# Rows spread over partitions in one pass: a rounded high part and a low part stacked in 40 rows, instead of full-precision matmuls

## What is computed

```
p = x @ w_in                                # 2048 -> RWKV-7 | retention | mLSTM columns
o_rw  = group_norm(rwkv7_scan(..., kk * rsqrt(sum kk^2 per head), ...)) ...   # 8 heads of 64
o_ret = silu(gr) * (yr * rsqrt(mean yr^2 per head))                           # 6 heads of 128
o_ml  = sigmoid(om) * (hm * rsqrt(mean hm^2 per head)) * ml_norm              # 6 heads of 128
        # mLSTM: exp(dlog - m_i), exp(inter - m_i): one value per head and token
x1 = layernorm(ALPHA * x + concat(o_rw, o_ret, o_ml) @ w_out)
x2 = layernorm(ALPHA * x1 + (silu(x1 @ w_gate) * (x1 @ w_up)) @ w_down)
```

## Time and profile before

| | |
|---|---|
| median of 3 runs | 2909.44 us (2906.31 to 2909.49) |
| profiled execution: time, span | 2905.3 us, 2903.5 us |
| mean granted TensorE clock | 0.975 of full |
| PE busy, PEld busy | 96%, 93% of the span |
| DVE busy, ACT busy | 56%, 41% |
| DMA | 152 GB/s over the span |

### The profile page before, as it was taken

One profiled execution on the slowest core, in us unless ns is written; L12 is line 12 of the kernel. 1 busy time (PEld: TensorE's weight loads), 2 busy tenths in 40 slices (PEclk: granted clock), 3 DMA queues, 4 the chain that ended last, 5 costly groups with the idle time before them and its releaser, 6 DMA issues.

```text
span 2903.5 us, 56248 instructions
## 1 busy us (share of the span) xinstructions
PE 2796.0 (96%) x23683; PEld 2697.5 (93%) x23683; DVE 1615.6 (56%) x1674; ACT 1180.7 (41%) x1455; POOL 0.2 (0%) x4
## 2 busy tenths in 40 slices
PE   6999999999999999999999999999999999999995
PEld 5988898889999999999999999888999999999995
DVE  5546547559554545444585575455875545454444
ACT  4345333436333333333363453343553333333333
POOL 0000000000000000000000000000000000000000
PEclk9999999989999999999999999989999999999997
DMA  5625334436666566555564543342666565655551
GB/s 158 195 85 156 89 89 136 125 112 187 185 177 179 175 180 176 178 179 170 179 196 140 163 114 89 83 131 73 187 188 180 174 181 174 180 179 179 173 181 60
DMA packets 278664, 445.02 MB, mean 153 GB/s; under 512 B 45124, under 2 KB 75646, under 8 KB 278182
## 3 DMA queue, kind: packets, MB, share of 16 engines
q1 hardware_dynamic: 276888, 439.29, 50.8%
q10 hardware_dynamic: 1600, 3.12, 0.3%
HBM read 430.58 MB, written 11.78 MB: 152 GB/s over the span
## 4 chain that ended last, share of the span: by engine, by line
PE 91%; DVE 5%; ACT 3%; issue 1%; DMA 0%; ACTq 0%; DVEq 0%
PE psum L644 19%; PE psum L645 19%; PE psum L643 19%; PE psum L676 7%; PE psum L677 6%; PE psum L678 6%; ACT w_hi L1215 1%; DVE w_lo L1589 1%; PE psum L877 1%; PE psum L666 1%; PE psum L667 1%; PE psum L668 1%; PE psum L867 1%; PE psum L1039 1%; PE psum L1024 1%
## 5 line engine op out<-in xcount | busy, mean ns | idle before, releaser
L1585 DVE TENSOR_TENSOR w_lo<-w_raw,w_hi 128x1024 fp32r<-128x1024 f32 x496 | 606.1, 1225 | 705.5 <-ACT w_hi L1202 703.8
L1202 ACT ACTIVATE w_hi<-w_raw 128x1024 fp32r<-128x1024 f32 x508 | 538.9, 1061 | 929.6 <-PE psum L645 920.4
L643 PE MATMUL psum<-x_hi,w_lo 128*128 128x264 f32 (+3 forms) x3072 | 878.8, 286 | 6.9 <-DVE x_lo L1787 6.9
L645 PE MATMUL psum<-x_hi,w_hi 128*128 128x264 f32 (+3 forms) x3072 | 879.5, 286 | 0.0
L644 PE MATMUL psum<-x_lo,w_hi 128*128 128x264 f32 (+3 forms) x3072 | 878.7, 286 | 0.0
L643 PEld LDWEIGHTS psum<-x_hi,w_lo 128*128 128x128 f32 x3072 | 582.1, 189 | 8.0 <-issue 7.3
L644 PEld LDWEIGHTS psum<-x_lo,w_hi 128*128 128x128 f32 x3072 | 581.3, 189 | 0.2
L645 PEld LDWEIGHTS psum<-x_hi,w_hi 128*128 128x128 f32 x3072 | 580.4, 189 | 0.0
L1589 DVE TENSOR_TENSOR w_lo<-w_raw,w_hi 128x1024 fp32r<-128x1024 f32 x304 | 369.0, 1222 | 247.0 <-ACT w_hi L1215 226.3
L1215 ACT ACTIVATE w_hi<-w_raw 128x1024 fp32r<-128x1024 f32 x292 | 304.9, 1056 | 299.2 <-PE psum L678 236.3
L676 PE MATMUL psum<-x_hi,w_lo 128*128 128x264 f32 (+1 forms) x1376 | 416.0, 302 | 6.3 <-ACT p_ml L1242 4.5
(11 more groups left out here) (444 smaller groups left out, 2605.3 us busy)
## 6 DMA issues: line engine op xcount, KB each, us to landing
w_raw<-in_w_in SPq DMA_DIRECT2D x192, 512.0 KB, 3.7
w_raw<-in_w_gate SPq DMA_DIRECT2D x176, 512.0 KB, 3.7
w_raw<-in_w_up SPq DMA_DIRECT2D x176, 512.0 KB, 3.8
w_raw<-in_w_down SPq DMA_DIRECT2D x176, 512.0 KB, 4.1
w_raw<-in_w_out SPq DMA_DIRECT2D x64, 512.0 KB, 3.9
w_raw<-in_w_in SPq DMA_DIRECT2D x16, 262.0 KB, 2.8
r_sample<-in_state_ret SPq DMA_DIRECT2D x6, 512.0 KB, 8.4
out_s_ret<-r_sample SPq DMA_DIRECT2D x6, 512.0 KB, 5.5
```

What stands on the lines that cost most here:

```text
L643: mm(out, w1, bh[:, k, 0:nt], start=(k == 0), stop=False)
L645: last = mm(out, w0, bh[:, k, 0:nt], start=False, stop=(k == last_k))
L1202: A(wh[:, j, :, :], raw[:, j, :, :], ACT.Copy).then_inc(S.hi_ready, 1)
L1585: TT(wl[:, j, :, :], raw[:, j, :, :], wh[:, j, :, :].bitcast(F32), ALU.subtract).then_inc(S.lo_ready, 1)
```

## The change

The table of selectors gets 40 rows: rows 0 to 7 as before, zeros, and the same eight rows again as rows 32 to 39. It is loaded as `selectors_loaded` and cast once to fp32r by DVE. A set of n rows is now kept twice in a tile of 40 rows: its rounded high part in rows 0 to n-1 and what is left of it in rows 32 to 32+n-1, with zeros between. One fp32r matmul of 38 or 40 rows with the doubled selector gives the sum of both parts in each output. The tile is `row_parts` for the norms and `m_row_parts` (three sets) for the mLSTM's rows. `invert` does the reciprocal, the rounding and the subtraction in turn, each waiting for the one before it. ACT computes two of the exponentials a second time, rounded, as the high parts. Cut to its core, the diff is:

```diff
-    sel = np.zeros((RW_HEADS, AH + 4, 128), f)
+    sel = np.zeros((32 + RW_HEADS, AH + 4, 128), f)
...
+    sel[32:] = sel[0:RW_HEADS]
...
-    sel = put("selectors", [RW_HEADS, AH + 4, 128])
+    sel = put("selectors", [32 + RW_HEADS, AH + 4, 128], F32R)
...
+    parts = at("row_parts", P_END + T * 4, [32 + RW_HEADS, T], F32R)
+    mparts = at("m_row_parts", P_X, [32 + AH, 3, T], F32R)
...
# PE: attention's spread and spread1 (h in 4, AH: the same), kks and gnsp, spread_m, spread_e
-                    last = mm(ps[:, 4 + h, 0:T], sel[0:AH, h, :], ln_s[0:AH, :], start=True, stop=True)
+                    last = mm(ps[:, 4 + h, 0:T], sel[0:32 + AH, h, :], parts[0:32 + AH, :], start=True, stop=True)
...
-                    last = mm(ps[:, 4 + b, 0:T], sel[:, AH + b, :], ln_s[0:RW_HEADS, :], start=True, stop=True)
+                    last = mm(ps[:, 4 + b, 0:T], sel[:, AH + b, :], parts[:, :], start=True, stop=True)
...
-                    last = mm(ps[:, 4 + h // 2, SEQ * (h % 2):SEQ * (h % 2) + SEQ], sel[0:AH, h, :], row(3)[:, 0:SEQ],
+                    last = mm(ps[:, 4 + h // 2, SEQ * (h % 2):SEQ * (h % 2) + SEQ], sel[0:32 + AH, h, :], mparts[:, 0, 0:SEQ],
                               start=True, stop=True)
                 last.then_inc(S.m_spread, 1)
                 bg.to('spread_e')
                 pe.wait_ge(S.m_exp_in, l + 1)
-                pe.wait_ge(S.m_rows_e, l + 1)
+                pe.wait_ge(S.m_rows_x, 2 * l + 2)
...
-                        mm(ps[:, 4 + p, SEQ * i:SEQ * i + SEQ], sel[0:AH, AH + p, :], row(r_)[:, 0:SEQ], start=True, stop=True)
+                        mm(ps[:, 4 + p, SEQ * i:SEQ * i + SEQ], sel[0:32 + AH, AH + p, :], mparts[:, 1 + i, 0:SEQ], start=True, stop=True)
...
# ACT
-                act.wait_ge(S.m_rows_x, l + 1)
+                act.wait_ge(S.m_rows_x, 2 * l + 1)
+                A(mparts[0:AH, 2, :], row(1), ACT.Exp)
                 A(row(1), row(1), ACT.Exp)
+                A(mparts[0:AH, 1, :], row(4), ACT.Exp)
                 A(row(4), row(4), ACT.Exp)
...
# DVE: invert replaces each v.reciprocal of ln_s (L1881, L2003, L2186)
+            def invert(n, sem):
+                x, hi = ln_s[0:n, :], parts[0:n, :]
+                own(v.reciprocal(x, x))
+                own(v.tensor_copy(hi, x))
+                TT(parts[32:32 + n, :], x, hi.bitcast(F32), ALU.subtract).then_inc(sem, 1)
...
+                if l == 0:
+                    dve.wait_ge(S.tables_loaded, 16 * 5)
+                    own(v.tensor_copy(sel[:, :, :], sel_raw[:, :, :]))
...
+                own(TS(parts[0:32, :], masks[0:32, 0:T], 0.0, None, ALU.mult))
                 bg = behind_ret(l)
...
+                own(TS(mparts[0:32, :, :], masks[0:32, 0:3 * T].rearrange("p (a t) -> p a t", t=T), 0.0, None, ALU.mult))
                 bg.to('gn')
...
                 dve.wait_ge(S.m_rows_m, l + 1)
+                then(v.tensor_copy(mparts[0:AH, 0, :], row(3)))
+                then(TT(mparts[32:32 + AH, 0, :], row(3), mparts[0:AH, 0, :].bitcast(F32), ALU.subtract))
                 then(TT(row(2), row(2), row(3), ALU.add))
...
+                dve.wait_ge(S.m_rows_e, l + 1)
+                TT(mparts[32:32 + AH, 1, :], row(4), mparts[0:AH, 1, :].bitcast(F32), ALU.subtract)
+                TT(mparts[32:32 + AH, 2, :], row(1), mparts[0:AH, 2, :].bitcast(F32), ALU.subtract).then_inc(S.m_rows_x, 1)
                 bg.to('spread_m')
```

More of the change, by code:

```diff
@@ L116, in constants @@
     return {'c_base': base, 'c_ident2': ident2, 'c_masks': masks, 'c_rot': rot, 'c_ret': ret, 'c_gam': gam,
-            'c_sel': sel.reshape(RW_HEADS, -1), 'c_sums': sums}
+            'c_sel': sel.reshape(32 + RW_HEADS, -1), 'c_sums': sums}
 def build(nc, a, o):
@@ L284, in build @@
     x_tok = at("x_rows", 0, [128, 3, D])
+    sel_raw = at("selectors_loaded", P_RW, [32 + RW_HEADS, AH + 4, 128])
     y_tok = at("y_rows", 0, [128, 3, D])
@@ L898, in attention @@
                 for h in range(4, AH):
-                    last = mm(ps[:, h, 0:T], sel[0:AH, h, :], ln_s[0:AH, :], start=True, stop=True)
+                    last = mm(ps[:, h, 0:T], sel[0:32 + AH, h, :], parts[0:32 + AH, :], start=True, stop=True)
                 last.then_inc(S.a_spread, 1)
@@ L1135, in _ @@
                 pe.wait_ge(S.rw_out, l + 1)
-                pe.wait_ge(S.m_rows_x, l + 1)
+                pe.wait_ge(S.m_rows_x, 2 * l + 1)
                 for c in range(NCH):
@@ L1144, in _ @@
                 pe.wait_ge(S.m_exp_in, l + 1)
-                pe.wait_ge(S.m_rows_e, l + 1)
+                pe.wait_ge(S.m_rows_x, 2 * l + 2)
                 for p in range(AP_):
-                    for i, r_ in enumerate((4, 1)):
-                        mm(ps[:, 4 + p, SEQ * i:SEQ * i + SEQ], sel[0:AH, AH + p, :], row(r_)[:, 0:SEQ], start=True, stop=True)
-                        last = mm(ps[:, 7, 16 * p + 8 * i:16 * p + 8 * i + 8], sel[0:AH, AH + p, :], row(r_)[:, SEQ:T],
+                    for i in range(2):
+                        mm(ps[:, 4 + p, SEQ * i:SEQ * i + SEQ], sel[0:32 + AH, AH + p, :], mparts[:, 1 + i, 0:SEQ], start=True, stop=True)
+                        last = mm(ps[:, 7, 16 * p + 8 * i:16 * p + 8 * i + 8], sel[0:32 + AH, AH + p, :], mparts[:, 1 + i, SEQ:T],
                                   start=True, stop=True)
@@ L1256, in _ @@
             act.dma_start(gam[:, :], a['c_gam']).then_inc(S.tables_loaded, 16)
-            act.dma_start(sel[:, :, :].rearrange("p a b -> p (a b)"), a['c_sel']).then_inc(S.tables_loaded, 16)
+            act.dma_start(sel_raw[:, :, :].rearrange("p a b -> p (a b)"), a['c_sel']).then_inc(S.tables_loaded, 16)
             act.dma_start(sums[:, :], a['c_sums']).then_inc(S.tables_loaded, 16)
@@ L1440, in _ @@
                 act.wait_ge(S.rw_kk_ss, l + 1)
-                A(ln_s[0:RW_HEADS, :], ln_m[0:RW_HEADS, :], ACT.Sqrt).then_inc(S.rw_kk_norm, 1)
+                A(ln_s[0:RW_HEADS, :], ln_s[0:RW_HEADS, :], ACT.Sqrt).then_inc(S.rw_kk_norm, 1)
                 for b in range(4):
@@ L1880, in attention @@
                 dve.wait_ge(S.a_std, n + 1)
-                v.reciprocal(ln_s[0:AH, :], ln_s[0:AH, :]).then_inc(S.a_inv, 1)
+                invert(AH, S.a_inv)
                 bg.to('spread')
@@ L2000, in _ @@
                 dve.wait_ge(S.rw_kk_sq, l + 1)
-                TS(ln_m[0:RW_HEADS, :], ps[0:RW_HEADS, 4, 0:T], 1e-24, None, ALU.max).then_inc(S.rw_kk_ss, 1)
+                TS(ln_s[0:RW_HEADS, :], ps[0:RW_HEADS, 4, 0:T], 1e-24, None, ALU.max).then_inc(S.rw_kk_ss, 1)
                 dve.wait_ge(S.rw_kk_norm, l + 1)
-                v.reciprocal(ln_s[0:RW_HEADS, :], ln_s[0:RW_HEADS, :]).then_inc(S.rw_kk_inv, 1)
+                invert(RW_HEADS, S.rw_kk_inv)
                 dve.wait_ge(S.rw_kk_raw, l + 1)
@@ L2185, in _ @@
                 dve.wait_ge(S.rw_gn_std, l + 1)
-                v.reciprocal(ln_s[0:RW_HEADS, :], ln_s[0:RW_HEADS, :]).then_inc(S.rw_gn_inv, 1)
+                invert(RW_HEADS, S.rw_gn_inv)
                 bg.to('gnsp')
```

## The result

| | median | runs | profiled execution: time, span | clock |
|---|---|---|---|---|
| before | 2907.86 us | 5 (2902.57 to 2909.49) | 2905.3, 2903.5 | 0.975 |
| changed | 2889.12 us | 5 (2884.76 to 2891.22) | 2889.2, 2887.5 | 0.977 |

The changed kernel is faster: ratio 0.9935, 95% interval [0.9923, 0.9947], which is 18.7 us by the medians. The forecast was 19.4 us less, a median of 2890 us.

A forecast was written before the change was run, and what follows sets the result against it. PE was taken to bound the kernel, busy 96% of the span. Savings of 7.54 us per layer, 15.1 in two, plus 4.3 from the clock gave 19.4 less: a median of 2890 us, range 2878 to 2902.

The forecast's parts named there:

- What bounds the kernel: PE, busy 96% of the span: a microsecond saved there counts, except where PE soon stands still for another engine.
- The price of a rounded matmul: At all six spreads: 0.122 us for each fp32r selector matmul, as for the filler's, instead of 0.492 in fp32.
- The additions: `invert` adds some 0.8 us, two ACT exponentials 0.64; zeroing and the table's cast cost nothing on the path.
- Retention: Retention's spreads: 1.25 us saved per layer, about 0.4 of `spread`'s 1.48 and all 0.85 of `spread1`.
- kks, 0: At kks: PE gains only 0.7 us, lost again at its next wait, L971, so 0 per layer.
- gnsp, -0.1: At gnsp: later ACT exponentials delay L2189 by 0.1 to 0.2 us, PE waits for `p_ml`; -0.1 per layer.
- spread_m, spread_e: The mLSTM's row spreads: no PE wait near, so the full 2.04 and 2.87 us per layer are saved.
- mLSTM: mLSTM's attention: `spread` saves 1.48 us per layer; `spread1`'s 0.85 only lengthens PE's wait for L666.
- The clock, 4.3: Three half-clock stretches behind spread_m and spread_e would be gone with the shorter fp32 runs, saving 4.3 us.
- The signs of being wrong: Selector matmuls of 0.25 us or more, half-clock stretches where none were, or PE waiting for `w_lo` in the filler.
- the clock gives nothing back: Rival, chance 0.19: longer waits open as many half-clock stretches as are won, leaving 15.1 us saved, 2894.

The follow-up runs named there:

- rows_128: The changed kernel with selectors and row sets filled up with zeros to 128 rows: 2886.10 us, ratio 0.9935 to the kernel before.
- adds_only: The kernel before plus all the change's additions on DVE and ACT, every selector matmul left fp32: 2907.44 us against 2905.87, ratio 1.0005.
- before_later_lo: The kernel before with one `w_lo` of DVE behind kks in layer 0 issued later, nothing else: 2899.33 us against 2908.21, ratio 0.9978.
- repeated: The changed kernel with each selector matmul of spread_m and spread_e issued four times: 2911.21 us against 2908.21 for the kernel before, ratio 1.0017.
- no_kks: The changed kernel with kks alone left in fp32, without its additions: 2889.37 us, ratio 0.9942 to the kernel before.
- later_lo_no_kks: The changed kernel with layer 0's `w_lo` behind kks issued later and kks in fp32 without additions: 2880.85 us against 2908.21 before, ratio 0.9915.
- later_lo: The changed kernel with one `w_lo` of DVE behind kks in layer 0 issued later: 2884.82 us against 2908.21 before, ratio 0.9930.
- rwkv_only: The kernel before with only kks and gnsp in the rounded format: 2910.89 us against 2905.87, ratio 1.0018.

## Why the prediction was right

- **What bounds the kernel**: right. PE's own stream decides, and a saving counts unless PE waits soon after.
- **The price of a rounded matmul**, 0.122: right within a run (0.12), too low at its ends. The first and last of a run take 0.22 and 0.21 to the next start; `rows_128` shows that this is the change between 128 and 40 rows. Four cost 0.67 and not 0.49, spread_m's six 0.90 and not 0.73. spread_e's twelve cost 1.47 and not 1.15, the larger part of it because a pair with an 8-column matmul takes 0.23 and not the estimated 0.19. Together this is most of the 1.7 us between 15.1 and 13.4.
- **The additions**: 0.78 for `invert` (0.8 taken), hidden at the attentions, on PE's path at kks (0.65 of wait), and `adds_only` bears out that all of them together cost little (1.6 us by the medians, at most 4 by the interval).
- **Retention**: 1.13 and 1.16 of 1.25, with the new wait at L903 (0.72 where 1.1 was expected).
- **kks, 0**: right in both layers, and the wait grew at the place named. But I took the longer wait to be free, and in layer 0 it wasn't: the half clock moved from ahead of it to behind it and took 0.86. The missing stretch at 309 gave 1.3 back, which the new wait of 1.26 at L1003 took again, so the retention's 0.85 was gone. No term stood for that.
- **gnsp, -0.1**: right in both layers, by the way predicted (two exponentials, then `w_hi`, `w_lo`, L2210).
- **spread_m, spread_e**: right but for the price above.
- **mLSTM**: right in size. The saving of `spread1` (0.64) is lost at L1159, which waits 0.59 us for `o_lo`, a step ahead of the L670 that I had named; L670's own wait is unchanged at 2.23.
- **The clock, 4.3**: the three stretches are gone, and they gave 1.5, 1.6 and some 1.5 us, so the step was right, though its reason was only half right: a long run of selector matmuls, not the fp32 format. What it left out is that others come and go. In the first profile 6.2 us were won behind spread_m and spread_e (with a fourth stretch at 1951), 5.3 lost in the four rows of the table with "none", and 1.7 won outside the table; in the second profile of the same program the balance is 4.4 us better. The forecast of 4.3 lies between 2.6 and 7.0, and that it came out right within a microsecond owes something to chance.
- **The signs of being wrong**: one of the three came true. Half-clock stretches turned up where none were, behind L670 in both layers, at 624.3 and 2023.8. They are not clearly the change's doing: the wait there is 2.23 us in both kernels, and `adds_only` and `before_later_lo`, in which every selector matmul is fp32, have half clock there in layer 0 as well (from 631.4 and 625.1).

The rival "the clock gives nothing back" (15.1 us) is the one that the first profile comes nearest to. The Trainium skill, "TensorE: Matmul & The Clock Gate", section "HAM oscillation", lays the throttling to idle time between bursts. Here a half-clock stretch does stand behind the waits of 5.25 and 2.23 us; that at 528.7 in `repeated` has no idle time ahead of it, and behind the 2.23 us of the kernel before there is none, so the rule is not the whole of it.

**What stays open.** Why the parts don't add up (8.2 against 18.7 us), and why `no_kks` is no faster than the whole while `later_lo_no_kks` is faster than `later_lo`. Totals of half clock differ from kernel to kernel by more than the effects of a place, and two profiles of one program by 10 us, so I take it for the clock; no run shows it. Nor is it shown what costs `rwkv_only` its 5 us.

## What to carry to other kernels

Before a saving on the busiest engine is counted, look for its next wait and follow that chain to its head: if the head is not the place that gets faster, the saving is gone, and a longer wait can even cost a little clock (0.6 to 0.8 us here). Such a chain can be worth more than the instruction: moving one filler operation of another engine out of it gave 4 to 9 us in the kernel before, though on top of the change too little to tell. Short row tables are cheap to spread in a rounded format as high and low part, in one matmul at a quarter of the price, where the extra operations on the rows have slack. And a difference of under 5 us here can't be read from one profile, since half-clock stretches come and go at the same place in the program.

## What the runs showed of the hardware

- A matmul of 38 or 40 rows and 264 columns in fp32r takes 0.12 us, as one of 128 rows; in fp32 with 6 or 8 rows 0.49. The matmul at each end of a run where the row count changes (128 to 40 and back) takes 0.1 us more.
- TensorE's clock fell to half in the middle of an unbroken run of 38-row matmuls (a run from 524.91, the clock at half from 528.6, in `repeated`).
- The same program had half-clock stretches of 123.0 and of 133.2 us in all in two profiles, with 4.4 us between the spans.
- The same wait of PE, of 2.4 to 2.8 us some 170 us ahead of the end, stands in all 14 profiles. The clock fell to half behind it in five and stayed at full in nine.
